# Two blocks of a transformer on one core: the dilated heads' preparation moved in among the first projection, and the experts' gather and scatter as sums of float32r parts

## What is computed

```python
def moe_swiglu(h, w_router, b_router, w1, w3, w2):
    ...
    for e in range(N_EXPERTS):
        out = out + gate[..., e:e + 1] * swiglu(h, w1[e], w3[e], w2[e])
```

## Time and profile before

| | |
|---|---|
| median of 3 runs | 2530.77 us (2529.77 to 2531.41) |
| the profiled execution | 2527.76 us |
| its span | 2526.4 us |
| PE busy | 2410.9 us, 95% |
| DVE, ACT, POOL busy | 1791.6, 1227.3, 390.5 us |
| even layer's mixer up to the dilated attention | about 47 to 167 us of the span |
| experts, first piece to last | 1497 to 2513 us of the span |
| one expert (the third) | 127.9 us |

### The profile page before, as it was taken

One profiled execution on the slowest core, in us unless ns is written; L12 is line 12 of the kernel. 1 busy time (PEld: TensorE's weight loads), 2 busy tenths in 40 slices (PEclk: granted clock), 3 DMA queues, 4 the chain that ended last, 5 costly groups with the idle time before them and its releaser, 6 DMA issues.

```text
span 2526.4 us, 27664 instructions
## 1 busy us (share of the span) xinstructions
PE 2410.9 (95%) x11091; PEld 1790.7 (71%) x11093; DVE 1791.6 (71%) x2019; ACT 1227.3 (49%) x1453; POOL 390.5 (15%) x434
## 2 busy tenths in 40 slices
PE   6987999999999999999999989999999999999998
PEld 2455797644579875454898658787878787878786
DVE  4576577585578755355665358888888888888887
ACT  1142453223145321222443247676767676767675
POOL 1035371131047010153220000000000000000000
PEclk9978999997999999899999999999999999999999
DMA  7631477642247875204565349999999999898995
GB/s 303 274 150 51 167 267 295 246 150 117 108 167 273 313 299 206 92 1 166 215 226 210 146 146 335 353 340 348 340 347 340 353 337 361 332 367 320 368 346 214
DMA packets 50671, 631.01 MB, mean 250 GB/s; under 512 B 8695, under 2 KB 9384, under 8 KB 12712
## 3 DMA queue, kind: packets, MB, share of 16 engines
q1 hardware_dynamic: 44192, 619.47, 65.1%
q10 hardware_dynamic: 3960, 6.97, 0.8%
q0 software_dynamic: 2384, 2.73, 0.3%
HBM read 625.47 MB, written 3.67 MB: 249 GB/s over the span
## 4 chain that ended last, share of the span: by engine, by line
PE 83%; DVE 9%; ACT 3%; issue 2%; DMA 2%; POOL 1%; ACTq 0%; SPq 0%; DVEq 0%; POOLq 0%
PE psum L1137 18%; PE psum L1138 18%; PE psum L1139 18%; PE psum L1032 4%; PE psum L1005 4%; PE psum L2462 3%; DVE sbuf L702 2%; PE psum L2456 2%; PE psum L1221 2%; PE psum L2044 1%; PE psum L742 1%; PE psum L2953 1%; PE psum L1172 1%; PE psum L3021 1%; PE psum L3049 1%
## 5 line engine op out<-in xcount | busy, mean ns | idle before, releaser
L1138 PE MATMUL psum<-ring_r,sc_r 128*128 128x512 f32 x1688 | 666.0, 395 | 0.0
L1132 DVE TENSOR_TENSOR ring_r<-ring,sbuf_r 128x2048 fp32r<-128x2048 f32 (+1 forms) x287 | 537.4, 1877 | 177.1 <-ACT sbuf_r L1123 175.5
L1123 ACT CAST sbuf_r<-ring 128x2048 fp32r<-128x2048 f32 (+1 forms) x287 | 445.3, 1555 | 343.2 <-PE psum L1139 258.4
L1132 DVE TENSOR_TENSOR ring_r<-ring,sc_r 128x2048 fp32r<-128x2048 f32 (+1 forms) x243 | 478.1, 1973 | 134.9 <-ACT sc_r L1123 133.8
L1123 ACT CAST sc_r<-ring 128x2048 fp32r<-128x2048 f32 (+1 forms) x243 | 398.4, 1642 | 268.2 <-PE psum L1139 233.6
L1137 PE MATMUL psum<-sbuf_r,sc_r 128*128 128x512 f32 (+1 forms) x1148 | 428.3, 373 | 4.2 <-DVE sc L2786 3.4
L1138 PEld LDWEIGHTS psum<-ring_r,sc_r 128*128 128x128 f32 x1688 | 317.4, 188 | 73.0 <-issue 3.1
L702 DVE SCALAR_TENSOR_TENSOR sbuf<-ring,sbuf 128x512 f32<-128x512 f32 x404 | 327.9, 819 | 22.3 <-DMA ring<-in_t_ada 16.8
L1139 PE MATMUL psum<-sbuf_r,sc_r 128*128 128x512 f32 x860 | 340.2, 396 | 0.0
L1137 PE MATMUL psum<-sc_r 128*128 128x512 f32 x828 | 333.3, 403 | 0.6 <-DVE sc_r L2985 0.6
L1139 PE MATMUL psum<-sc_r 128*128 128x512 f32 x828 | 324.2, 392 | 0.0
(11 more groups left out here) (333 smaller groups left out, 2871.0 us busy)
## 6 DMA issues: line engine op xcount, KB each, us to landing
ring<-in_t_moe SPq DMA_DIRECT2D x168, 2048.0 KB, 7.8
ring<-in_t_ada SPq DMA_DIRECT2D x48, 2048.0 KB, 9.4
ring<-in_t_mlp SPq DMA_DIRECT2D x32, 2048.0 KB, 8.3
ring<-in_t_win SPq DMA_DIRECT2D x17, 2048.0 KB, 9.6
ring<-in_t_ffn SPq DMA_DIRECT2D x16, 2048.0 KB, 8.0
ring<-in_t_out SPq DMA_DIRECT2D x7, 2048.0 KB, 8.3
ring<-in_t_bias SPq DMA_DIRECT2D x2, 2048.0 KB, 10.0
...
```

Of the source, the lines that this page charges most:

```text
L1123: p.act.e.copy(p.r(hi), src).then_inc(*p.sig("high", st.tag, n))
L1132: p.dve.e.tensor_tensor(p.r(src), src, p.r(hi), ALU.subtract).then_inc(*p.sig("lowp", st.tag, n))
L1138: e.matmul(out, l[0], r[1], start=False, stop=False)
```

## The change

It has two parts.

In the even layer, the statistics of the dilated queries and keys are split into two rounds (`dve_stats`, `act_squares`) and these and three of DVE's four rotations are issued among the projection's tiles j = 3 to 5; POOL's follow the same results. PE turns the queries ahead of `uq` and the keys between `uq` and `ukv`. The tables for the rotations (`dve_setup` and ACT's sines) are made in j = 1 instead of j = 2. Tile 9 of `ada` is loaded after the latents' weights, its eight products are done in the attention's rounds (two a round in rounds 1 to 5), and its sums beside those of tiles 10 and 11 in the output projection.

In the experts, the normed rows XN are split once into two float32r parts (`act_rows_high`, `dve_rows_parts`), and the one-hot matrices are rounded too. One gather of 32 float32r matmuls of 256 columns serves two experts; it is issued for even experts only. The gates leave the one-hot matrix: they come by two float32 matmuls of one column (into GS), and DVE applies gate and gate row as it takes the result out of PSUM (`dve_rows_out`). ACT rounds this result, DVE subtracts, and the scatter is eight float32r matmuls of 512 columns, two pieces later than before; DVE adds what it gives straight to X, after the product of j = 0. The last expert's scatter stays in float32. AM and `dve_fold` go.

```diff
-        self.TABS = region(1856)
+        self.TABS = wide[:, 448:2304]
+        self.XNH = v3(wide[:, 0:2048], 2)
...
         loads = [("ada", q) for q in range(4)]
-        for j in range(6):
-            loads += [("win0", j), ("ada", 4 + j)]
-        loads += [("uq", 0), ("uq", 1), ("ukv", 0), ("ukv", 1), ("ada", 10), ("ada", 11), ("out0", 0), ("ada", 12),
+        loads += self.among("win0", range(6), 1, range(4, 9))
+        loads += [("uq", 0), ("uq", 1), ("ukv", 0), ("ukv", 1), ("ada", 9), ("ada", 10), ("ada", 11), ("out0", 0), ("ada", 12),
                   ("out0", 1)]
...
-        self.AM = v3(sc[:, 13312:15360], 2)
+        self.XSB = sc[:, 13312:15360].rearrange("p (e k n) -> p e k n", e=2, k=8)
+        self.YSH = sc[:, 13312:14336]
         self.FG, self.YS = GROW[0], GROW[1]
-        self.XS = v3(GROW[1], 8)
-        self.PM = [v3(GROW[2][:, 256 * i:256 * i + 256], 2) for i in range(2)]
-        self.PG = v3(GROW[2][:, 512:768], 2)
+        self.PM, self.PMR = (v3(GROW[2][:, 512 * i:512 * i + 512], 2) for i in range(2))
...
+        self.GS = [sc[:, 15524 + i:15525 + i] for i in range(2)]
...
+def pe_heads(p, tag, base):
+    for h0 in (0, 6):
+        p.pe.wait_ge(*p.at("rotD", (tag, h0)))
+        p.pe.wait_ge(*p.at("rotG", (tag, h0)))
+    pe_turn(p, tag, lambda b, c: p.U[:, b, base + 128 * c:base + 128 * c + 128], 6, [0, 1])
...
+def dve_stats(p, tag):
+
+    c = 24 * (tag == "dk")
+    for b in range(2):
+        p.dve.wait_ge(*p.at("dsq", tag, b))
+        p.dve.e.tensor_reduce(p.SQ[:, c + 12 * b:c + 12 * b + 12], v3(p.SQT0[b], 12), X_AXIS, ALU.add).then_inc(
+            *p.sig("dss", tag, b))
+    p.dve.wait_ge(*p.at("dss", tag, 1))
+    dve_rstd(p, tag, p.SQ[:, c:c + 24], p.RQ[:, c:c + 24], 64)
...
+def act_squares(p, tag):
+    base, first = (DK, 4) if tag == "dk" else (DQ, 2)
+    for u in range(first, 10 if tag == "dk" else 6):
...
+        p.act.e.activation(v3(p.SQT0[b], 12), v3(p.U[:, b, base:base + 768], 12), ACT.Square).then_inc(*p.sig("dsq", tag, b))
+    c = 24 * (tag == "dk")
+    act_root(p, tag, p.SQ[:, c:c + 24])
...
         if j:
             pe_sums(p, 4 + j)
-    pe_sums(p, 10)
     p.pe.wait_ge(*p.at("latents"))
...
+    for ev in (turn_at(p, "lq", 0), turn_at(p, "lq", 1), turn_at(p, "lkv", 0)):
+        p.pe.wait_ge(*ev)
+    pe_heads(p, "dq", DQ)
...
+    p.pe.wait_ge(*turn_at(p, "dq", 1))
+    p.pe.wait_ge(*turn_at(p, "dq", 2))
+    pe_heads(p, "dk", DK)
...
-    for tag, base in (("dq", DQ), ("dk", DK)):
...
-        pe_turn(p, tag, lambda b, c: U[:, b, base + 128 * c:base + 128 * c + 128], 6, [0, 1])
...
-    p.pe.wait_ge(*p.at(*moved(p, p.accs[9][0])))
+    p.pe.wait_ge(*p.at(*moved(p, p.accs[8][0])))
...
     for j in range(6):
+        if j == 3:
+            dve_stats(p, "dq")
         dve_put(p, "u0", 2 * j, U[:, 0, 512 * j:512 * j + U0[j]], U0[j])
-        if j == 2:
-            dve_setup(p)
+        if j >= 3:
+            tag, h0 = (("dq", 0), ("dq", 6), ("dk", 0))[j - 3]
+            if j == 5:
+                dve_stats(p, "dk")
+            dil_rotate(p, p.dve, "D", 0, tag, h0)
+        if j < 5:
+            dve_products(p, 8, 5 + j)
         if j == 1:
             dve_latents(p)
-        dve_products(p, 8, 5 + j)
+            dve_setup(p)
         if j:
             dve_columns(p, 4 + j)
-    dve_columns(p, 10)
     dve_turn(p, "lq", p.HT, 3, [0], p.QLN)
...
     dve_turn(p, "dq", p.QT2, 6, [0, 1])
+    dil_rotate(p, p.dve, "D", 0, "dk", 6)
...
         if i:
-            dve_products(p, 1, 13)
+            dve_products(p, 1 + (i < 6), 13)
...
         dve_products(p, 1, 13)
+    dve_columns(p, 10)
...
     for j in range(6):
+        if j in (3, 5):
+            act_squares(p, "dq" if j == 3 else "dk")
         act_put(p, "u0", 2 * j + 1, U[:, 1, 512 * j:512 * j + U0[j]], U0[j])
-        if j == 2:
...
+            r = v3(p.sc[:, 19264:19328], 2)
+            act_sine(p, "sin", p.SIN, r)
+            act_sine(p, "cos", p.COS, r)
         if j:
             act_gates(p, 4 + j)
-    act_gates(p, 10)
...
-    act_root(p, "d", p.SQ[:, 0:48])
+    act_turn(p, "dq", p.QT2, 6, [0, 1])
...
+    act_turn(p, "dk", p.KT2, 6, [0, 1])
...
-    act_turn(p, "dq", p.QT2, 6, [0, 1])
-    act_turn(p, "dk", p.KT2, 6, [0, 1])
...
-    pool_seed(p, 13)
-    p.pool.wait_ge(*p.at("rstd", "d"))
-    for tag, base, col, name in (("dq", DQ, 0, "dil_q_norm"), ("dk", DK, 12, "dil_k_norm")):
+    pool_seed(p, 11)
+    for tag in ("dq", "dk"):
+        p.pool.wait_ge(*p.at("rstd", tag))
         for h0 in (0, 6):
...
+            dil_rotate(p, p.pool, "G", 1, tag, h0)
+        pool_seed(p, 12 + (tag == "dk"))
...
+def dve_rows_parts(p):
+
+    p.dve.wait_ge(*p.at("tp", "n7", 3))
+    for b in range(2):
+        p.dve.wait_ge(*p.at("rowhigh", "n7", b))
+        xn = p.XN[:, b, :]
+        p.dve.e.tensor_tensor(p.r(xn), xn, p.r(p.XNH[:, b, :]), ALU.subtract).then_inc(*p.sig("rowlow", "n7", b))
...
+    for b in range(2):
+        p.act.wait_ge(*p.at("xnD", 7, b))
+        p.act.wait_ge(*p.at("xnA", 7, b))
+        p.act.e.copy(p.r(p.XNH[:, b, :]), p.XN[:, b, :]).then_inc(*p.sig("rowhigh", "n7", b))
...
     e = p.pe.e
-    i = x % 2
-    if step in (1, 2):
+    one = lambda b: p.PM[:, b, 128 * (x % 2):128 * (x % 2) + 128]
+    if step in (1, 2) and x % 2 == 0:
         c4 = step - 1
-        ps = p.bank[2 + c4]
-        p.pe.wait_ge(*p.at("onehot", tag, x))
-        p.pe.wait_ge(*p.at(*held[2 + c4]))
-        for c in range(4):
-            for b in range(2):
-                ins = e.matmul(ps[:, 128 * c:128 * c + 128],
-                               p.XN[:, b, 128 * (4 * c4 + c):128 * (4 * c4 + c) + 128], p.PM[i][:, b, :],
-                               start=(b == 0), stop=(b == 1))
-        ins.then_inc(*p.sig("gather", tag, x, c4))
-        held[2 + c4] = ("gathered", tag, x, c4)
+        p.pe.wait_ge(*p.at("gates", tag, "rows", x))
+        for r in range(2):
+            ps = p.bank[2 + r]
+            p.pe.wait_ge(*p.at("rowlow", "n7", 1))
+            p.pe.wait_ge(*p.at(*held[2 + r]))
+            for c in range(2):
+                k = 4 * c4 + 2 * r + c
+                for b in range(2):
+                    for m, xn in enumerate((p.XNH, p.XN)):
+                        ins = e.matmul(ps[:, 256 * c:256 * c + 256], p.r(xn[:, b, 128 * k:128 * k + 128]),
+                                       p.r(p.PMR[:, b, :]), start=(b == 0 and m == 0), stop=(b == 1 and m == 1))
+            ins.then_inc(*p.sig("gather", tag, x, 2 * c4 + r))
+            held[2 + r] = ("gathered", tag, x, 2 * c4 + r)
     if step == 3:
         p.pe.wait_ge(*p.at(*held[2]))
         for b in range(2):
-            ins = e.transpose(p.bank[2][:, 128 * b:128 * b + 128], p.PG[:, b, :], p.IDENT)
+            e.transpose(p.bank[2][:, 128 * b:128 * b + 128], one(b), p.IDENT)
+        for b in range(2):
+            ins = e.matmul(p.bank[2][:, 256:257], one(b), p.GATE[:, b, x:x + 1], start=(b == 0), stop=(b == 1))
         ins.then_inc(*p.sig("gateT", tag, x))
         held[2] = ("gates", tag, x)
...
+    if step == 0 and x % 2 == 0:
...
+        for m in range(2):
+            for b in range(2):
+                ins = e.tensor_scalar(p.PM[:, b, 128 * m:128 * m + 128], p.IOTA, p.POSN[:, b, x + m:x + m + 1],
+                                      p.MASK[:, b, x + m:x + m + 1], ALU.is_equal, ALU.mult)
         ins.then_inc(*p.sig("onehot", tag, x))
...
+    if step == 0 and i == 0:
+        p.act.wait_ge(*p.at("onehot", tag, x))
+        if x:
+            p.act.wait_ge(*p.at("gather", tag, x - 2, 3))
+        e.copy(p.r(p.PMR), p.PM).then_inc(*p.sig("gates", tag, "rows", x))
...
+        for r in range(2 * step - 2, 2 * step):
+            p.act.wait_ge(*p.at("gather", tag, x, r))
+            for c in range(2):
+                k = 2 * r + c
+                ins = e.activation(p.XSB[:, :, k, :], v3(p.bank[2 + r % 2][:, 256 * c:256 * c + 256], 2), ACT.Identity,
+                                   bias=p.MODC[3][2][:, k:k + 1], scale=p.MODC[3][3][:, k:k + 1])
+            ins.then_inc(*p.sig("gathered", tag, x, r))
...
+        e.copy(p.r(p.HS[i][0][:, k, :]), p.XSB[:, i, k, :]).then_inc(*p.sig("rowhigh", tag, x, step - 1))
...
+        e.copy(p.GS[i], p.bank[2][:, 256:257])
+        g = p.GE[i] if x == 7 else p.r(p.GE[i])
+        e.copy(g, p.bank[2][:, 0:256]).then_inc(*p.sig("gates", tag, x))
...
+def dve_rows_out(p, tag, x):
+    for h in range(2):
+        cols = slice(512 * h, 512 * h + 512)
+        if x and h == 0:
+            p.dve.wait_ge(*p.at("scatter", tag, x - 1, 3))
+        p.dve.wait_ge(*p.at("gates", tag, x))
+        p.dve.e.scalar_tensor_tensor(out=p.YS[:, cols], in0=p.bank[h], scalar=p.GS[x % 2], in1=p.GROW[3][:, cols],
+                                     op0=ALU.mult, op1=ALU.mult).then_inc(*p.sig("rowsD", tag, x, h))
+
+
+def act_rows_out(p, tag, x):
+    for h in range(2):
+        cols = slice(512 * h, 512 * h + 512)
+        p.act.wait_ge(*p.at("rowsD", tag, x, h))
```

(93 more changed lines are left out.)

80 lines of the change are left out of this document (20 added, 60 removed).

## The result

Four runs of the changed kernel: 2501.98 us median (2497.47 to 2507.9), against 2531.09 (2529.77 to 2531.79) for four of the kernel before. Ratio 0.9887, 95% interval [0.9864, 0.991]. The forecast was 2505 with a range from 2494 to 2517. The profiled execution took 2499.86, with a span of 2498.6, so 27.8 us less span than before; the sum in the prediction was 25.6.

A forecast was written before the change was run, and what follows sets the result against it. PE was taken to bound the kernel, busy 95% of the span, except before the dilated attention. Experts -19.2, their start +0.8, end -1.9 and even layer -5.3 sum to -25.6 us, from 2530.77 to 2505; range 2494 to 2517.

The forecast's parts named there:

- even layer: Stages before the experts: attention starts 9.6 us sooner, products in its rounds cost 3.0, tile 9's sums 1.3; together -5.3 us.
- parts' chain: Experts: PE waits at each of seven scatters for the result's and pieces' parts, 0.5 each; +3.5 us, bounds 0 to 14.
- one-hot: Experts: the one-hot matrix's stall of PE's transposes, 7 x 0.42 us out and 3 x 0.55 in; -1.3 us.
- gate scalars: Experts: two float32 matmuls of one column cost 0.5 us for each of seven experts; +3.3 us.
- scatter: Experts: eight float32r matmuls of 512 columns take 1.84 us instead of 3.44 at seven scatters; -11.2 us.
- gather: Experts inside the loop: 32 float32r matmuls at 3.8 us, three times, replace gathers totalling 24.9 us; -13.5 us.
- end: After the last expert: four DVE adds, each behind a float32 scatter pair, let the norm start near 2518.1; -1.9 us.
- (a): Rival: PE's clock stays up in the dilated attention's first rounds, some 4 us less; 2501 us, chance 0.12.
- (b): Rival: the even layer gives nothing, as products, later loads and slower rotations eat PE's gain; 2510.5 us, chance 0.15.
- (c): Rival: the parts come 2 us late at each scatter because DVE's line is too full; 2515.5 us, chance 0.08.
- (d): Rival: slower than before, the low parts over 4.2 us late in each expert's first pieces; 2536 at 5 us, chance 0.03.
- (e): Rival: float32r gathers run no faster per column, so the time stays within 0.2%; chance 0.02.

The follow-up runs named there:

- the execution with late tiles: The changed kernel with the old even layer, so the experts' edits alone against the kernel before: 2514.63 us, ratio 0.9932.
- the early scatter: The changed kernel with each scatter back at its old place, two pieces into the next expert instead of four: 2558.91 us, ratio 1.0126 to the kernel before.
- its half alone: The kernel before with the even layer's edits alone, experts as before: 2522.24 us, against 2529.86 beside it, ratio 0.9964.

## Why the prediction came out right, point by point

The direction, the main mechanisms and the total held: 25.6 forecast, 27.8 by the spans. The total is closer than its terms, and that is in part luck: terms that came out better than forecast add up to 7.8 (even layer 3.8, parts' chain 2.6, one-hot 1.2, gate scalars 0.2), and terms that came out worse to 5.6, of which 3.3 are a wait at the gather that the prediction had at nothing. By terms, in us:

| term | forecast | measured |
|---|---|---|
| scatter, 7 times | -11.2 | -11.2 (3.44 to 1.83) |
| parts' chain wait | +3.5 | +0.9 |
| gather | -13.5 | -13.4, and +3.3 of waits |
| one-hot stall | -1.3 | -2.5 |
| gate scalars | +3.3 | +3.1 |
| others in the loop | 0 | +1.3 |
| experts' loop | -19.2 | -18.5 |
| start of the experts | +0.8 | +0.9 |
| end | -1.9 | -1.1 |
| even layer | -5.3 | -9.1 |

**Scatter and gather** were priced from rows of the same shape and came within 0.1 us: 0.23 a matmul of 512 columns, and 16 matmuls of 256 in 1.91, 0.119 each, against 0.118 from the earlier trace rows. Among the others are PE's transposes of the hidden values in even experts: where a half of the gather used to stand ahead of them they now start 0.2 late, in the pieces of j = 4 and j = 5, eight times, 1.7 in all.

```profile
1791.31 0.39 PE L1140 MATMUL psum<-sc_r 128*128 128x512 f32 x1
1791.69 0.66 PE L3100 MATMUL psum<-sbuf,sc 128*128 128x128 f32 x4
```

**The parts' chain** is shown as a mechanism by the early scatter (+53 us in the experts) and by the execution with late tiles. Its size depends on a tile's arrival: 0.9 in the profiled execution, 0.3 to 4.9 in the others. 3.5 lies inside, in its upper part.

**One-hot matrix.** I kept a stall of 0.55 for the three experts with four operations, which is what piece 13 shows (3.73 for 3.16), and took 0.42 for the removed ones from the visible wait; the piece that holds it was 0.6 longer. The mistake of the step was another: it looked only at the product behind the four operations, not at ACT's copy behind them. "ACT's copy of one column and of PM lies beside PE" was wrong. The copy waits up to 3.4 us in ACT's queue, two weight roundings stand behind it, and the delay returns at the gather as three waits of 1.1. The step should have named what is queued behind the copy.

**End.** The norm's first step comes 5.2 behind the last scatter's start instead of 6.5; I had 4.6:

```profile
2486.22 1.41 DVE L3074 SCALAR_TENSOR_TENSOR sbuf<-psum,sc,sbuf 128x512 f32<-128x512 f32 x2 [6.91 <-PE psum L1140]
...
2487.03 3.70 PE L3130 MATMUL psum<-sbuf,sc 128*128 128x512 f32 x8 [0.84 <-DVE sbuf L3074]
...
2489.80 2.48 DVE L3271 TENSOR_TENSOR sbuf<-sbuf,psum 128x512 f32<-128x512 f32 x4 [2.17 <-PE psum L3130]
...
2492.20 0.15 DVE L3434 TENSOR_SCALAR sbuf<-sbuf 128x1 f32<-128x1 f32 x1
```

DVE's first add starts 2.77 behind the first scatter matmul; in the trace of before the first step was 1.17 behind the earlier trace rows. Between the two on DVE's stream lies the jump to the closing block, which before fell into 3.8 idle us and now follows DVE's own work. That is argued from the program, no run tried it. The step that failed is the pace: I had the four adds each behind its own scatter pair, and they start late and then run in one piece, 2.48 us for four.

**Even layer**, the term that was most off. The attention starts 11.3 sooner, not 9.6: 1.5 of the difference is the projection, which I took over at 16.47 although part of that row ran at the lower clock, and which takes 7.91 and 7.03 now. Then I charged 3.0 for the products in the rounds. The run with them back speaks for that price within the stage (47.0 against 49.9 us for five), as does the one with products in DVE's idle stretch (48.4 for two fewer). But the stage of before was no clean base: it took 48.8 in the first trace and 50.7 in the execution with the old even layer and the new experts, same code. Between the two profiled executions the stage grew by 1.0 only. Nor is the -9.1 itself firm: two executions with the old even layer and seven with the new one, compared at one and the same product of DVE near 299 us, differ by 8.8 to 14.2, pair by pair. Tile 9's sums and the handover cost 1.1 for 1.3.

**The rivals.** (a), the clock stays up in the first rounds: the clock did start at 1.00, but it fell at 157.8 with PE busy (5.90 of 6.30 us at a mean of 0.59), and ahead of that it had been busy 7.56 of 8.40 us from 147.0 and 1.60 of 1.60 from 155.4, at 1.00. So the sentence that the low clock follows the idle stretch does not hold for this trace, and for the trace of before only from 156.6 on: there too the clock had fallen at 136.1, with PE busy 3.68 of the 5.00 us from 130 on. By the Trainium skill, page "TensorE: Matmul & The Clock Gate" (What's actually happening), the throttled clock is the default and activity releases it; this trace agrees in the attention's start at 1.00, and shows that small matmuls with PE nearly always busy did not keep it. More to the point, the rival's price was wrong: the time at the low clock does not set the stage. Busy time of the stage in the run with the early scatter, whose even layer is the changed kernel's:

```profile
154.70:204.50 49.80, 36.49 (x181) 26.62 (x181) 35.32 (x69) 17.83 (x34) 24.32 (x34) 0.83 0.30 121
```

The mean clock is 0.83 here and 0.73 in the changed kernel's trace, PE is busy 4.5 us less, and the stage takes the same 49.8. (b), the even layer gives nothing: refuted by its half alone. (c), the parts 2 us late at each scatter, and (d), over 4.2 us late: neither in any execution as a whole; single scatters had up to 2.3, and (d)'s mechanism is what the early scatter shows. (e): refuted by the matmuls' distances.
